# Who splits the weight slabs: ScalarE and VectorE instead of GpSimd from the first feed-forward on, and a ring of three split slabs

## What is computed

```python
# layer 0: mixer = HGRN2 (8 heads of 128); layer 1: mixer = stick-breaking attention (16 heads of 64)
h = h + mixer(rmsnorm(h, g_mix))
gate, up = split(rmsnorm(h, g_ffn) @ w_ffn_in)        # 1024 -> 2 x 2816
h = h + (silu(gate) * up) @ w_ffn_out                 # 2816 -> 1024
h = h + (p[l] @ w_ple_in) * sigmoid(rmsnorm(h, g_ple) @ w_ple_gate)
# after layer 0: K, V = split(rmsnorm(h, g_kv) @ w_kv), used by layer 1
y = rmsnorm(h, g_final)
```

## Time and profile before

| | us |
|---|---|
| median of 3 runs | 4825.13 (4817.6 to 4828.23) |
| the profiled execution, whole | 4813.35 |
| its span, first to last instruction | 4811.6 |
| TensorE matmuls busy | 3997.2 (83%) |
| VectorE busy | 2563.2 (53%) |
| ScalarE busy | 1048.3 (22%) |
| GpSimd busy | 876.8 (18%) |
| mean granted TensorE clock | 0.845 of full speed |

### The profile page before, as it was taken

The page is one execution under the profiler, slowest core; times in us unless marked ns, Lnnn a source line. Parts: engine busy times, 40 slices in busy tenths (PEclk is TensorE's granted clock), DMA queues, the critical chain, the costliest instruction groups (busy, mean ns, idle before and its releaser), DMA issues. The chain is left out here.

```text
span 4811.6 us, 63502 instructions
## 1 busy us (share of the span) xinstructions
PE 3997.2 (83%) x22632; PEld 3767.1 (78%) x22632; DVE 2563.2 (53%) x4678; ACT 1048.3 (22%) x1862; POOL 876.8 (18%) x536
## 2 busy tenths in 40 slices
PE   6777777775899999978987888888889899999975
PEld 5666776664899999978986777777779899999975
DVE  4667656557544445565133555665552555444465
ACT  3212222212200000033022333443330200000032
POOL 2111111110222222223320000000002222222222
PEclk9777887876999999989996666666669999999987
DMA  2000010100111111111222222222222111111111
GB/s 76 32 23 27 31 36 31 36 22 24 36 43 39 44 39 44 39 53 62 91 105 87 92 92 92 77 73 90 67 70 87 35 44 39 39 44 39 44 49 62
DMA packets 76295, 259.06 MB, mean 54 GB/s; under 512 B 11810, under 2 KB 15906, under 8 KB 75810
## 3 DMA queue, kind: packets, MB, share of 16 engines
q1 hardware_dynamic: 68418, 233.73, 15.4%
q10 hardware_dynamic: 7776, 24.11, 1.3%
HBM read 231.46 MB, written 26.35 MB: 54 GB/s over the span
## 5 line engine op out<-in xcount | busy, mean ns | idle before, releaser
L1250 PE MATMUL psum<-xh,wh 128*128 128x352 f32 x4032 | 1337.3, 332 | 138.6 <-DVE xl L848 91.8
L1254 PE MATMUL psum<-xl,wh 128*128 128x352 f32 x4032 | 1320.4, 327 | 0.0
L1255 PE MATMUL psum<-xh,wl 128*128 128x352 f32 x4032 | 1320.0, 327 | 0.0
L509 POOL CAST wh<-raw 128x1024 fp32r<-128x1024 f32 x244 | 269.2, 1103 | 3826.1 <-issue 1446.8
L1250 PEld LDWEIGHTS psum<-xh,wh 128*128 128x128 f32 x4032 | 780.9, 194 | 149.6 <-issue 142.2
L832 DVE TENSOR_TENSOR work<-psum,rstd 128x352 f32<-128x352 f32 x408 | 211.5, 523 | 1124.8 <-PE psum L1255 1103.7
L1254 PEld LDWEIGHTS psum<-xl,wh 128*128 128x128 f32 x4032 | 781.4, 194 | 1.1
L1255 PEld LDWEIGHTS psum<-xh,wl 128*128 128x128 f32 x4032 | 778.3, 193 | 0.0
L839 DVE TENSOR_TENSOR h<-h,psum 128x352 f32<-128x352 f32 x1272 | 568.9, 508 | 122.0 <-PE psum L1255 121.6
L511 POOL TENSOR_TENSOR wl<-raw,wh 128x1024 fp32r<-128x1024 f32 x244 | 595.5, 2440 | 19.5
L1250 PE MATMUL psum<-ah,wh 128*128 128x352 f32 x1344 | 461.8, 344 | 144.8 <-DVE h L839 117.4
(11 more groups left out here) (194 smaller groups left out, 4609.1 us busy)
## 6 DMA issues: line engine op xcount, KB each, us to landing
raw<-in_wstream SPq DMA_DIRECT2D x244, 512.0 KB, 3.5
h<-in_kT_cache SPq DMA_DIRECT2D x64, 512.0 KB, 6.5
h<-in_v_cache SPq DMA_DIRECT2D x48, 512.0 KB, 3.9
work<-in_v_cache SPq DMA_DIRECT2D x16, 512.0 KB, 4.5
h<-in_xT SPq DMA_DIRECT2D x3, 1408.0 KB, 11.3
out_kT_out<-work ACTq DMA_DIRECT2D x8, 528.0 KB, 2.7
out_vT_out<-work ACTq DMA_DIRECT2D x8, 528.0 KB, 2.7
qT_scratch<-work ACTq DMA_DIRECT2D x8, 528.0 KB, 2.7
```

The source lines that it names most:

```text
L509: nc.gpsimd.tensor_copy(wh[:, slot, :], raw[:, slot, :]).then_inc(split_hi, 1)
L1250: ins = mm(out, wh[:, slot, ws], mh, start=first, stop=False)
L1254: mm(out, wh[:, slot, ws], ml, start=False, stop=False)
L1255: return mm(out, wl[:, slot, ws], mh, start=False, stop=last)
```

## The change

From the first feed-forward on GpSimd splits nothing. ScalarE makes the high part (`hi`) and VectorE the low part (`lo`), at fixed places in their queues: one pair per slab, two slabs ahead at the start of a stage. `raw` keeps its two slots; `wh` and `wl` get three, and the wait before a split is for the first matmul of slab i-2 instead of slab i-1, for GpSimd in the mixer too. Of a `w_ple_in` slab only the first 256 columns (`PSLAB`) are split. The loops over the tiles of PLE, of `staged`, of `stage_tiles` and of `products` are written out instead of being hardware loops. In K, V, Q and attention's output product one `hi` and one `lo` stand before each tile, and after attention two pairs go ahead of them. At the end of the mixer half of the last head's adds are moved behind the new wait.

```diff
+WRING = 3
+PSLAB = PK * P
-        wh = sb("wh", [P, 2, SLAB], F32R)
-        wl = sb("wl", [P, 2, SLAB], F32R)
+        wh = sb("wh", [P, WRING, SLAB], F32R)
+        wl = sb("wl", [P, WRING, SLAB], F32R)
@@ GpSimd @@
-                wait(pool, w_used, i - 1 if not isinstance(i, int) or i > 2 else 0)
+                wait(pool, w_used, i - WRING + 1)
...
-            pool.wait_ge(pe_z, 16 * PAIRS)
-            rest = (NSLAB - BEFORE) // 2
-            with pool.Fori(0, rest) as i, looped(i, rest, n=(n, 2)):
-                split(0)
-                split(1)
@@ ScalarE @@
+            def hi(width=SLAB):
+                if casts.n >= limit[0]:
+                    return
+                i = casts.up()
+                r, slot = (casts.n - 1) % 2, (casts.n - 1) % WRING
+                act.wait_ge(landed[r], ((casts.n - 1) // 2 + 1) * 16 + casts.off * 8)
+                wait(act, w_used, i - WRING + 1)
+                nc.scalar.activation(wh[:, slot, 0:width], raw[:, r, 0:width], ACT.Copy).then_inc(split_hi, 1)
...
+            act.wait_ge(w_ready, N_A)
+            hi()
+            hi()
...
             def gated(buf, down):
+                hi()
                 gate_groups(ACT.Silu)
+                hi()
                 for g in range(G):
                     act.wait_ge(a_prod, prods.up())
                     nc.scalar.activation(ah[:, buf, cols(g)], up_s[:, cols(g)], ACT.Copy).then_inc(a_hi, 1)
-                units.up(G + (KT * G if down else 0))
+                units.up(G)
+                if down:
+                    hi()
+                    units.up(KT * G)
...
-                with act.Fori(0, KT) as i, looped(i, KT, un=(units, 6)):
+                for n in range(KT):
+                    hi()
                     gate_groups(ACT.Sigmoid)
+                    hi(PSLAB if n < KT - 1 else SLAB)
                     units.up(G)
...
@@ VectorE @@
+            def lo(width=SLAB):
+                if lows.n >= limit[0]:
+                    return
+                i = lows.up()
+                r, slot = (lows.n - 1) % 2, (lows.n - 1) % WRING
+                dve.wait_ge(split_hi, i)
+                nc.vector.tensor_tensor(wl[:, slot, 0:width], raw[:, r, 0:width], flat(wh[:, slot, 0:width]),
+                                        ALU.subtract).then_inc(w_ready, 1)
             def gated(buf, down):
+                lo()
                 evac(gate_s)
+                lo()
                 wait(dve, a_ready, his.at())
                 evac(up_s)
                 dve.wait_ge(unit_free, units.at())
...
                 for n in range(2 if down else 0):
                     add_to_h(n)
+                if down:
+                    lo()
                 for g in range(G):
                     dve.wait_ge(a_hi, his.up())
                     nc.vector.tensor_tensor(al[:, buf, cols(g)], up_s[:, cols(g)], flat(ah[:, buf, cols(g)]),
                                             ALU.subtract).then_inc(a_ready, 1)
...
-                with dve.Fori(0, KT) as n, looped(n, KT, un=(units, 6), ga=(gates, 3), own=(own, 3)):
+                for n in range(KT):
+                    lo()
                     dve.wait_ge(unit_free, units.at())
                     evac(gate_s)
+                    lo(PSLAB if n < KT - 1 else SLAB)
...
...
@@ VectorE, end of the mixer @@
-                for n in range(KT):
+                for n in range(KT if ahead else KT // 2):
                     add_to_h(n)
...
+            dve.wait_ge(w_ready, N_A)
+            depth[0] = G
+            lo()
+            for n in range(2):
+                add_to_h(KT // 2 + n)
+            lo()
+            for n in range(2, KT // 2):
+                add_to_h(KT // 2 + n)
+            depth[0] = SETS
@@ TensorE @@
-                return (slabs.n - 1) % 2
+                return (slabs.n - 1) % WRING
...
-    nc = _bacc.Bacc("TRN2", target_bir_lowering=False, num_devices=1)
+    nc = _bacc.Bacc("TRN2", target_bir_lowering=False, num_devices=1, dynamic_dma_scratch_size=2048)
```

More of the change, by code:

```diff
@@ L500, in _, with split @@
             n = Count()
-            def split(slot):
+            def split():
                 i = n.up()
-                arrived = ((n.n - 1) // 2 + 1) * 16 + n.off * 8
-                pool.wait_ge(landed[slot], arrived)
-                wait(pool, w_used, i - 1 if not isinstance(i, int) or i > 2 else 0)
+                r, slot = (n.n - 1) % 2, (n.n - 1) % WRING
+                pool.wait_ge(landed[r], ((n.n - 1) // 2 + 1) * 16 + n.off * 8)
+                wait(pool, w_used, i - WRING + 1)
                 pool.sem_inc(split_go, 1)
-                nc.gpsimd.tensor_copy(wh[:, slot, :], raw[:, slot, :]).then_inc(split_hi, 1)
+                nc.gpsimd.tensor_copy(wh[:, slot, :], raw[:, r, :]).then_inc(split_hi, 1)
                 pool.wait_ge(split_hi, i)
-                nc.gpsimd.tensor_tensor(wl[:, slot, :], raw[:, slot, :], flat(wh[:, slot, :]), ALU.subtract)\
+                nc.gpsimd.tensor_tensor(wl[:, slot, :], raw[:, r, :], flat(wh[:, slot, :]), ALU.subtract)\
                     .then_inc(w_ready, 1)
-            split(0)
-            split(1)
[L516 to L519, removed]
+            for _ in range(6):
+                split()
+            rounds = N_A // 6 - 1
+            with pool.Fori(0, rounds) as i, looped(i, rounds, n=(n, 6)):
+                for _ in range(6):
+                    split()
             pool.wait_ge(stg_out[0], 16 * STORES)
@@ L587, in _ @@
             norm(G_MIX0)
+            casts, limit = Count(), [BEFORE]
+            casts.n = N_A
+            def hi(width=SLAB):
[6 more added lines that the diff above has]
+                nc.scalar.activation(wh[:, slot, 0:width], raw[:, r, 0:width], ACT.Copy).then_inc(split_hi, 1)
             forget, decays, exponents, kts, outs, osums, vts, states, heads, ons = [Count() for _ in range(10)]
@@ L689, in ffn @@
                 rounds = FT // 2 - 1
-                with act.Fori(0, rounds) as i, looped(i, rounds, un=(units, 60), pr=(prods, 6)):
+                with act.Fori(0, rounds) as i, looped(i, rounds, un=(units, 60), pr=(prods, 6), ca=(casts, 6)):
                     gated(0, True)
                     gated(1, True)
+                hi(PSLAB)
                 units.up(KT * G)
             def gated(buf, down):
+                hi()
                 gate_groups(ACT.Silu)
+                hi()
                 for g in range(G):
@@ L715, in staged @@
                 dst_t = dst.rearrange("(n p) t -> n p t", p=P)
[L716 to L720, removed]
+                for n in range(KT):
+                    hi()
+                    act.wait_ge(unit_free, units.up(G))
+                    act.dma_start(dst_t[n, :, :], stage[:, n % 2, :]).then_inc(stg_out[n % 2], 16)
             ffn(G_FFN0)
@@ L794, in _ @@
                             .then_inc(o_hi, 1)
-            units.up(KT * G)
+            act.wait_ge(pe_z, 16 * PAIRS)
+            limit[0] = NSLAB
+            hi()
+            hi()
+            for n in range(KT):
+                hi()
+                units.up(G)
             ffn(G_FFN1)
@@ L1053, in ffn @@
                 rounds = FT // 2 - 1
-                with dve.Fori(0, rounds) as i, looped(i, rounds, un=(units, 60), ga=(gates, 6), hi=(his, 6)):
+                with dve.Fori(0, rounds) as i, looped(i, rounds, un=(units, 60), ga=(gates, 6), hi=(his, 6),
+                                                      lo=(lows, 6)):
                     gated(0, True)
@@ L1057, in ffn @@
                 for n in range(KT):
+                    if n == 2:
+                        lo(PSLAB)
                     add_to_h(n)
@@ L1071, in ple @@
                         did(nc.vector.tensor_tensor(gate_s[:, cols(g)], gate_s[:, cols(g)], src[:, 0:GW], ALU.mult))
-                        hv = h[:, bass.ds(n, 1), cols(g)].rearrange("p o t -> p (o t)")
-                        nc.vector.tensor_tensor(hv, hv, gate_s[:, cols(g)], ALU.add).then_inc(unit_free, 1)
+                        nc.vector.tensor_tensor(h[:, n, cols(g)], h[:, n, cols(g)], gate_s[:, cols(g)], ALU.add)\
+                            .then_inc(unit_free, 1)
             tiles = Count()
             def stage_tiles(scale):
[L1078 to L1088, removed]
+                for n in range(KT):
+                    lo()
+                    t = tiles.up()
+                    for g in range(G):
+                        src = unit_bank()
+                        dve.wait_ge(unit_done, units.up())
+                        if g == 0:
+                            wait(dve, stg_out[n % 2], (t - 1) // 2 * 16)
+                        nc.vector.scalar_tensor_tensor(stage[:, n % 2, cols(g)], src[:, 0:GW], scale,
+                                                       rstd[:, cols(g)], ALU.mult, ALU.mult).then_inc(unit_free, 1)
+            dve.wait_ge(w_ready, N_A)
[3 more added lines that the diff above has]
+                add_to_h(KT // 2 + n)
+            lo()
```

(11 more changed lines are left out.)

3 lines of the change are left out of this document (2 added, 1 removed).

## The result

| | before | after |
|---|---|---|
| median, us | 4824.4 (4 runs, 4817.6 to 4828.2) | 4770.7 (4 runs, 4767.1 to 4772.3) |
| the profiled execution | 4813.35 | 4767.14 |
| span | 4811.6 | 4765.1 |
| TensorE granted clock, mean | 0.845 | 0.836 |

The ratio is 0.9889, 95% interval 0.9872 to 0.9906: 53.7 us faster by medians, 46.5 us between the two spans. Forecast were 87.5 us off, 4737, with a range up to 4770. The sign was right and nearly two fifths of the gain are missing.

A forecast was written before the change was run, and what follows sets the result against it. TensorE, 83% busy, was taken as the bound, so only its waits or lower-clock time could be won: -64.7 - 8.5 - 17.0 + 0.35 + 1.9 + 0.4 = -87.5 us, giving a median of 4737, range 4707 to 4770.

The forecast's parts named there:

- GpSimd blocks the multiplies; without it the first stall goes.: Feed-forward down product: GpSimd's split stretches VectorE's up-by-gate multiplies to 4.09 us; freed, TensorE's wait for add 0 disappears.
- `lo` 1 and 2 are hidden, `lo` 3 leaves 2.0 us.: Feed-forward tile: two low parts cost TensorE nothing; the third delays add 6, a 2.0 us stall; 1.54 us a tile gained.
- The dips cost 0.27 us a tile ... so I let a quarter stay: 8.5 us gained.: Feed-forward: brief falls of TensorE's clock cost 11.3 us in all; the shorter stall keeps a quarter, gaining 8.5 us.
- the clock keeps falling: Feed-forward rival, 15%: the clock falls in every tile, 0.5 us instead of 0.27; -69 us, 4756.
- PLE by the ring, 17 us.: Per-layer-embedding loops: three slots end TensorE's wait for the split; turns of 14.4 instead of 15.82 us, 17.0 us gained.
- Mixer 0, "at the same instants": HGRN2 mixer: GpSimd's splits still start when TensorE takes a slab, so the change was taken as 0.
- Changes of stage, +2.65.: Between stages: +1.9 us mixer to feed-forward, +0.4 attention to output product, +0.35 last PLE turns; KV and Q hidden.
- Range: Whole kernel: 4707 (a mixer that gets free too lies below) to 4770 us (slower rival and no gain above).
- A median of the new kernel should stand likewise: Whole kernel: the new median lies 11.8 us above its profiled execution, as before; 4726 becomes 4737.

The follow-up runs named there:

- the ring alone: The changed kernel, but GpSimd splits all 244 slabs at full width, with three slots and loops written out: 4807.5 us, ratio 0.9981 to the kernel before.

## Why the prediction was wrong, step by step

- *GpSimd blocks the multiplies; without it the first stall goes.* Right: 1.40 us for 4.09, first add at 2.17 us into down as worked out. Copies on ScalarE and subtractions on VectorE cost 1.04 and 1.22 us, as in attention. The Trainium skill's rule on the shared interfaces ("SBUF — State Buffer", "Who interferes with whom") names VectorE with two SBUF inputs and GpSimd as the pair that excludes each other; these rows agree.
- *`lo` 1 and 2 are hidden, `lo` 3 leaves 2.0 us.* Right to 0.05 us; a tile without a fall is 36.5 us (36.56).
- *"The dips cost 0.27 us a tile ... so I let a quarter stay: 8.5 us gained."* This step failed, in both of its factors. I took the price of a fall from the rows of before, 0.5 us, though there it lay ahead of a wait for VectorE that hid two thirds of it; and I took the number, a quarter of the old, from nothing but the shorter stall, though after 2.0 us the clock still fell in more than half of the tiles. In its place: 24 of 40 tiles at 1.6 us = 38 us lost, where before 19 at 0.5 = 10 were. By 40 tiles: 40 x 1.58 = 63 us won on the tile (38.10 to 36.52), +10.6 for the old falls, -38 for the new: 36, the measured number. Without that term the forecast would stand: the version without falls in which the stall is 1.45 us has loops of 722.6 and 719.8 us, and half a microsecond a tile more makes some 731, for the 36.56 x 20 = 731 worked out.
- The rival "the clock keeps falling" had the right cause with the wrong size: it priced a fall at 0.5 us in every tile, 4756. With 1.6 us in 24 of 40, thus 40 us in 42 tiles, and all of the old 11.3 gone, it gives -64.7 - 11.3 + 40 - 17.0 + 2.65 = -50, 4775 on the median of 4825. The Trainium skill ("TensorE: Matmul & The Clock Gate", "A second HAM failure mode: psum-queue depth-cycling") tells of a kernel in which short idles between groups, while it cycled through PSUM banks, made the clock swing. The 24 tiles after a stall of 2.0 us agree with that; the 40 with a stall of 0.85 us and the 40 with 1.45, at a clock of 1.00, show that here such idles alone weren't enough.
- *PLE by the ring, 17 us.* Right, 18.3, and 17.9 of it without moving the split. The first turn of each PLE began at the lower clock; it gained nothing in the first and 0.5 us in the second, where the forecast had 0.
- *Mixer 0, "at the same instants".* Wrong for the third slab: with a third slot its split no longer waits until TensorE takes slab 2, and it ran into the first norm. It cost 2.7 us up to the third token group; the first output slab came 3.3 us later, and how much of that is the blocking is not settled.
- *Changes of stage, +2.65.* +2.3 measured. The end of the mixer, with two `lo` between its adds, cost the 1.9 worked out.
- *Range.* It ended at 4770, 0.7 us below the result, since a fall's price was taken as known. Bounded from both sides, it is 0.5 us by the row and 1.7 for 3.4 us at half speed with TensorE busy. At 1.7 in each of 42 tiles the sum is -64.7 - 11.3 + 71.4 - 17.0 + 2.65 = -19, and the upper end 4806.
- *"A median of the new kernel should stand likewise", 11.8 us above the profiled execution.* It stood 3.6 above. So the forecast is 41 us off between the profiled executions (4726 against 4767.1) and 34 between the medians; the 7 us between are luck.

## What to carry to other kernels

The price of a fall of the clock depends on what TensorE has to do after it: read it where TensorE is bound by itself, not where another engine paces it, because a change that removes the other wait also removes the cover. When a stall is being shortened, count the falls at each length: here the step from 2.0 to 1.45 us took 57 us from the two loops, the next, from 1.45 to 0.85, only 28. And before work is moved to another engine, look at what stands ahead of the instruction that others wait for: moving the split brought 54 us, and putting the two kinds of subtraction behind the adds another 116 by medians, 120 by the loops.

## What the runs showed of the hardware

- The clock fell after an idle of 2.0 us in 24 of 40 tiles and after 3.25 in 38, never after 1.45 or 0.85; it came 2.3 to 4.7 us after the idle had begun, after the 2.0 us ones always with TensorE busy again (0.3 to 1.1 us after their end), and lasted 3.4 us each time (6.8 in three tiles of the longest stall).
- A longer idle in another rhythm was not worse: after 2.56 us the clock fell in 19 and in 21 of 40 tiles of 38.1 us (before, and the ring alone) and in 16 of 40 tiles of 37.0. So the idle's length alone doesn't give the number of falls.
- A fall of 3.4 us cost 1.5 to 1.6 us where TensorE had nothing to wait for behind it, and 0.5 where a stall of 0.9 us followed.
- A VectorE multiply of 128x352 with both inputs in SBUF that met a GpSimd split ended 0.37 to 0.39 us after one of GpSimd's two instructions, in all 88 cases of the kernel before. Eight instructions of the first norm took 8.43 us beside three GpSimd operations, 5.47 beside one; eight of the same kind took 4.04 beside none.
